# A hybrid encoder layer on eight cores: one explicit order for the mixing stage, transposes moved to DMA, conv statistics by mask matmuls

## The chip, the cores and the metric

The kernel runs on the 8 cores of one Trainium2 chip, each core with one sequence of the batch; the cores exchange nothing. The metric is the device time of the slowest core in microseconds (us). The engines of a core are named as in the profile: PE (TensorE, matmuls), PEld (its weight loads), DVE (VectorE), ACT (ScalarE), POOL (GpSimd) and SP (SyncE, which here only issues DMAs). "SPq" is SP's instruction queue, "POOLq" that of POOL.

## The reference, cut to what matters

One layer over x of 2048 tokens by 1024 channels (per core), with 256 memory tokens:

```python
proj = x @ w_in        # -> conv GLU input 1024 | q 512 | k 128 | v 128 | memory q 512 | gates 3*1024
u = a * sigmoid(g)                                    # branch A: GLU, 512 channels
u = depthwise_conv(u, width 31) + dw_b
u = silu(layer_norm(u over channels, ln_g, ln_b));  y_conv = u @ w_conv_out
# branch B: 8 heads of 64, 2 kv heads, blocks of 128 queries that see 3 blocks of keys
p = softmax([q k^T / 8 + rel_bias, sink])[..., :-1];  y_attn = (p @ v) @ w_attn_out
# branch C: 4 heads of 128 over the 256 memory tokens
y_mem = softmax(q_mem km^T / sqrt(128)) @ vm @ w_mem_out
merged = sum_b sigmoid(gate_b + b_gate) * y_b
x1  = layer_norm(alpha * x + merged @ w_o, ln1)
out = layer_norm(alpha * x1 + (silu(x1 @ w_gate) * (x1 @ w_up)) @ w_ffn_out, ln2)
```

Matmuls run in bf16 with sums in f32.

## The kernel before, in words

The program is written engine by engine with hand-set semaphores: each engine executes its instructions in the order in which the Python code emits them, and a wait at the head of an engine's queue holds all that stands behind it. Inputs live transposed in SBUF (`xT`: channels on partitions), so a projection is a "group": 8 matmuls of 128x128 by 512 tokens into one PSUM bank (`group8`, L333, through the helper `mm`, L221).

Stages, in order:

- **Start.** Small constants are loaded by SP into one slot `s_small`; POOL loads the GLU weights of channel block 0 (`wglu`, gate and value halves in one DMA) and x of token quarter 0 in two halves. The first matmul is that of the attention bias table (`setup_bias`, L412), which waits for all small constants; the GLU groups of quarters 0 and 1 follow, then q, k and v of quarters 0 and 1.
- **Mixing stage**, tokens in four quarters k = 0..3. Its work comes as lists. *Mains*: projection groups (GLU gate `g_gate` and value `g_a`, q, k, v, memory q) and, for output block dp = 0, `c_main`: gate groups `c_gate` and branch projections `c_out`. *W*: windowed attention, per block n three score steps `w_S` (two 64-row matmuls, exp on ACT, bias product on DVE), a value step `w_V` per kv head (12 matmuls of 65 columns, then normalisation on DVE into `otm`), and `w_T` (L618): four PE transposes and a DVE copy into `qT`. *M*: memory attention, units of 512 tokens and one head: `m_S`, `m_V`, and `m_T` (L692): four PE transposes and a copy into `qmT`. *CV*: the conv chain of each quarter: four `conv_c` (L483, 32 matmuls of 32 columns each), `stats` (L503: sums over channels by matmuls with a matrix of ones, which also spreads them over all partitions), mean, variance, `sqrt` on ACT (a table of its own), four `recip` on DVE, `z0` and `fin` (normalise, tanh, product) into `U0`.
- `weave` (L804) and `merge_lists` (L793) mix these lists by weights: a side step is emitted when its share of the sides' weight is reached by the mains' share.
- **Conv inputs.** A conv unit i = 4k + c reads four shifted images of `U0`, made by 16 small DMAs that SP issues (`uq_issue`, L461). There are three buffers: the loads of unit i + 3 are emitted in `conv_c` of unit i and wait for it; they also wait for the GLU output of the next quarter.
- **Gates and outputs** for dp = 1, 2, 3 (`c_main` over four quarters each), nothing else beside them. POOL adds the branches and issues the weight loads; `cache_w1` lets POOL write a bf16 copy of the first FFN weight to HBM, in five large DMAs.
- **Output projection and first LayerNorm** (D): per block of 128 tokens `d_mm` (16 matmuls), `d_H` (residual, DVE, frees the two PSUM banks), `d_S` (sum of squares, ACT), `d_tiny` (DVE), `d_sqrt` (ACT), `d_recip` (DVE), `d_C` (two DVE passes, then a bf16 copy on ACT), `d_Tpe` (L1003: eight PE transposes) and `d_Tev` (L1014: ACT copy into `x1T`). The loop at L1087 interleaves the last of them with the first FFN steps.
- **FFN** (E): `e_step` runs two hidden blocks (32 matmuls; silu on ACT, product on DVE); after 11 steps the second matmul of that quarter follows, which waits for the product of the last block (`e_state["a"]`), then the second LayerNorm and the store.

PSUM has eight banks: during the mixing stage two pairs and four single ones, later a ring of eight.

Of the kernel before, what the change touches and what calls it, by code (L numbers as in the profile page):

```python
# [11 lines left out]
D = 1024  # L12
# [66 lines left out]
class Slot:  # L79
# [11 lines left out]
def _build(plan):  # L91
# [80 lines left out]
    dnt = nc.alloc_sbuf_tensor("dnt", [128, 2, 8], F32)  # L172

# [67 lines left out]
    otm = [V(171.75 + 0.5 * i, [128, 4, 64]) for i in range(4)]  # L241
# [4 lines left out]
    meanb = V(191.75, [128, 512], F32)  # L246
    rstdb = V(193.75, [128, 512], F32)
# [9 lines left out]
    s_small = new_slot("small")  # L257
# [21 lines left out]
    load_glu(0)  # L279
    load_xt(0)  # L280
    load_glu(1)
# [9 lines left out]
    t_eps = pool.run(lambda: nc.gpsimd.memset(eps_t[:, 1:2], 4.0 * LN_EPS))  # L291
    t_onesb = pool.run(lambda: nc.gpsimd.memset(ones_bf[:], 1.0))
# [183 lines left out]
    cst = {"cv": [[], [], [], []], "h": [[], [], [], []], "q": [[], [], [], []], "mean": [], "rstd": []}  # L476
    t_sT = {}

    def conv_steps(k):
# [23 lines left out]
        def stats():  # L503
            b, dd = banks.alloc(2)
            for c in range(4):
                t_a = mm(ps[:, b, :], ones_bf[:], cvh[c], c == 0, c == 3, [S["h", c], t_onesb, dd if c == 0 else None],
                         inc=(c == 3))
            for c in range(4):
                t_b = mm(ps[:, b + 1, :], ones_bf[:], sqb[c], c == 0, c == 3, [S["sq", c]], inc=(c == 3))
            cst["h"] = [[t_a]] * 4  # L510
            cst["q"] = [[t_b]] * 4
            S["mean"] = dve.run(lambda: nc.vector.tensor_scalar(
                out=meanb, in0=ps[:, b, :], scalar1=1.0 / 512, scalar2=None, op0=ALU.mult), [t_a, cst["mean"]])
            t_m2 = dve.run(lambda: nc.vector.tensor_tensor(out=rstdb, in0=meanb, in1=meanb, op=ALU.mult),
                           [S["mean"], cst["rstd"]])
            S["var"] = dve.run(lambda: nc.vector.scalar_tensor_tensor(
                out=rstdb, in0=ps[:, b + 1, :], scalar=1.0 / 512, in1=rstdb, op0=ALU.mult, op1=ALU.subtract), [t_b, t_m2])
            banks.release(b, S["var"], 2)

        def sqrt():  # L520
            S["sd"] = act.run(lambda: nc.scalar.activation(rstdb, rstdb, AF.Sqrt, bias=eps_t[:, 0:1]), [S["var"], t_eps])

        def recip(i):
            S["rs"] = dve.run(lambda: nc.vector.reciprocal(rstdb[:, 128 * i:128 * i + 128], rstdb[:, 128 * i:128 * i + 128]),  # L524
                              [S["sd"]])

        def z0(i):
            S["z0", i] = dve.run(lambda: nc.vector.tensor_tensor(out=cvs[i], in0=cvs[i], in1=meanb, op=ALU.subtract),
                                 [S["mean"], S["h", i]])

        def fin(c):
            t_z1 = dve.run(lambda: nc.vector.tensor_tensor(out=cvs[c], in0=cvs[c], in1=rstdb, op=ALU.mult),  # L532
                           [S["rs"], S["z0", c]])
            cst["rstd"] = [t_z1]
            t_z2 = dve.run(lambda: nc.vector.tensor_scalar(  # L535
                out=cvs[c], in0=cvs[c], scalar1=cvec[:, 4 + c:5 + c], scalar2=cvec[:, 8 + c:9 + c],
                op0=ALU.mult, op1=ALU.add), [t_z1, t_cvec])

            def fin_th():
# [3 lines left out]
                t_th = act.run(lambda: nc.scalar.activation(th2[r], cvs[c], AF.Tanh), [t_z2, th_free[r]])  # L543

                def fin_s():
                    t_sT[k, c] = dve.run(lambda: nc.vector.scalar_tensor_tensor(  # L546
                        out=U0[:, c, 512 * k:512 * k + 512], in0=th2[r], scalar=1.0, in1=cvs[c],
                        op0=ALU.add, op1=ALU.mult), [t_z2, t_th])
# [6 lines left out]
        for c in range(4):  # L555
            steps.append((1.7, lambda c=c: conv_c(c)))
        steps.append((0.1, lambda: None))
# [623 lines left out]
```

How the kernel before makes its waits and increments, by code:

```python
    def wait(self, deps):  # L45
        for tok in _flat(deps):
            if tok[0] == "E":
                _, src, v = tok
                k = id(src)
                if self.seen.get(k, 0) >= v:
                    continue
                self.seen[k] = v
                src.needed.add(v)
                if self.plan is not None:
                    self.eng.wait_ge(src.sem, src.vmap[v])
            else:
                sem, val = tok
                k = id(sem)
                if self.seen.get(k, 0) >= val:
                    continue
                self.eng.wait_ge(sem, val)
                self.seen[k] = val
# [1 line left out]
    def run(self, fn, deps=(), inc=True):  # L64
        self.wait(deps)
        ins = fn()
        if inc:
            self.v += 1
            if self.plan is None or self.v in self.plan[self.name]:
                ins.then_inc(self.sem, 1)
                self.real += 1
                self.vmap[self.v] = self.real
            return ("E", self, self.v)
        return None
# [61 lines left out]
    def dma(e, out, in_, slot, deps=()):  # L136
        e.wait(deps)
        e.eng.dma_start(out=out, in_=in_).then_inc(slot.sem, 16)
        slot.count += 16
        return slot.tok()
```

The softmax here doesn't subtract the row's maximum and nothing guards it: scores larger than these inputs give would overflow.

## Time and profile before

| | us |
|---|---|
| three timed runs, median | 1102.94 (1100.15, 1102.94, 1121.49) |
| the profiled execution, device time | 1101.29 |
| its span on the slowest core, first to last instruction | 1099.7 |
| the eight cores' spans | 1092.8 to 1099.7 |

The profile is of one execution on its slowest core. "Busy" counts time in which an engine executes; issuing a DMA, waiting and branching are not counted. "PEclk" is the granted share of TensorE's full clock. Some 1.6 us of the device time lie outside the span. Stretches of time are counted from the first instruction.

### The profile page before, as it was taken

What the parts mean: (1) busy time and instruction counts of PE and PEld (TensorE: products, weight loads), DVE (VectorE), ACT (ScalarE), POOL (GpSimd) and SP (SyncE); (2) the same over time, 40 slices, a digit from 0 to 9 for tenths busy, and PEclk for the clock granted to TensorE, in tenths of its full rate; (3) what the DMA queues carried; (4) which work ended last, traced back from release to release, by engine and by line L of the source; (5) the groups of instructions that cost most, each with busy time, mean ns of one, the idle gap of its engine ahead of it and who ended that gap; (6) DMA issues with size and microseconds to landing.
All of it is one profiled execution on the core that took longest, in us unless ns stands there. A gap on an engine that the chain in (4) does not pass through costs nothing.

```text
span 1099.7 us, 15676 instructions; the slowest of 8 cores (1092.8 to 1099.7 us)
## 1 busy us (share of the span) xinstructions
PE 1008.7 (92%) x5662; PEld 466.1 (42%) x5662; DVE 434.6 (40%) x789; ACT 359.4 (33%) x518; POOL 124.9 (11%) x156
## 2 busy tenths in 40 slices
PE   3999978546979999999999999999999999999996
PEld 1445434222435444444444444444444444444442
DVE  1325575417587222222235855143213322342224
ACT  1135544415645222222223798122111211121111
POOL 2100000000111433433330010000000000000000
PEclk9999989868989999999999999999999999999998
DMA  9990102550012895973049198405440444134401
GB/s 140 191 187 12 53 22 61 111 119 24 13 32 56 132 171 90 139 120 77 1 86 291 35 206 206 154 39 155 154 152 39 134 153 154 39 117 153 134 19 58
DMA packets 39467, 116.22 MB, mean 106 GB/s; under 512 B 7584, under 2 KB 15912, under 8 KB 38144
## 3 DMA queue, kind: packets, MB, share of 16 engines
q0 software_dynamic: 11136, 49.55, 25.8%
q1 hardware_dynamic: 28256, 65.67, 19.3%
q8 instruction: 47, 0.77, 0.3%
q14 instruction: 28, 0.23, 0.1%
HBM read 138.32 MB, written 19.93 MB: 144 GB/s over the span
## 4 chain that ended last, share of the span: by engine, by line
PE 83%; SPq 5%; DVE 5%; DMA 3%; ACT 3%; issue 2%; DVEq 0%; POOL 0%; ACTq 0%; POOLq 0%
PE ps L221 81%; SPq L138 5%; DMA arena<-arena 1%; DMA esink<-sinkp 1%; DVE arena L977 1%; ACT arena L935 1%; DVE arena L524 1%; DVE arena L532 1%; ACT arena L664 0%; ACT arena L1016 0%; PE ps L625 0%; PE ps L1008 0%; DVE arena L535 0%; DVE arena L956 0%; DVE arena L546 0%
## 5 line engine op out<-in xcount | busy, mean ns | idle before, releaser
L221 PE MATMUL ps<-arena 128*128 128x512 bf16 (+5 forms) x5372 | 989.3, 365 | 41.8 <-DMA arena<-arena 22.4
L221 PEld LDWEIGHTS ps<-arena 128*128 128x128 bf16 (+2 forms) x5372 | 447.6, 99 | 566.3 <-issue 94.6
L1046 DVE TENSOR_TENSOR arena<-ps,arena 128x512 bf16<-128x512 f32 x88 | 60.6, 691 | 201.0 <-PE ps L221 180.3
L768 DVE SCALAR_TENSOR_TENSOR arena<-arena,ps 128x512 f32<-128x512 f32 x96 | 65.9, 686 | 148.7 <-PE ps L221 148.7
L747 ACT ACTIVATE arena<-ps,bgate_sb 128x512 f32<-128x512 f32 x96 | 66.1, 688 | 168.8 <-PE ps L221 168.8
L1044 ACT ACTIVATE arena<-ps 128x512 f32<-128x512 f32 x88 | 51.4, 597 | 180.8 <-PE ps L221 180.7
L935 ACT ACTIVATE arena<-arena 128x1024 bf16<-128x1024 f32 (+1 forms) x32 | 33.9, 1058 | 140.4 <-DVE arena L1067 133.1
L775 POOL TENSOR_TENSOR arena<-arena 128x512 f32<-128x512 f32 x32 | 40.4, 1263 | 199.3 <-DVE arena L768 189.8
L138 POOL DMA_DIRECT2D out<-arena x16 | 8.5, 532 | 411.9 <-DVE arena L958 411.9
L587 ACT ACTIVATE arena<-ps 128x1024 bf16<-128x1024 f32 x46 | 46.8, 1023 | 8.3 <-PE ps L221 8.3
L780 POOL TENSOR_TENSOR arena<-arena 128x512 bf16<-128x512 f32 x32 | 40.8, 1274 | 61.2 <-DVE arena L768 56.6
L1067 DVE SCALAR_TENSOR_TENSOR arena<-arena,ps 128x1024 f32<-128x1024 f32 x16 | 19.5, 1221 | 67.2 <-PE ps L221 67.2
L958 DVE SCALAR_TENSOR_TENSOR arena<-arena,mvt 128x1024 f32<-128x1024 f32 x32 | 41.1, 1285 | 3.6
L956 DVE SCALAR_TENSOR_TENSOR arena<-arena,mvt 128x1024 f32<-128x1024 f32 x32 | 41.0, 1281 | 2.1 <-DVE mvt L952 0.4
L590 DVE TENSOR_TENSOR arena<-arena 128x1024 bf16<-128x1024 bf16 x46 | 35.0, 760 | 14.8 <-ACT arena L587 14.8
L330 ACT CAST arena<-ps 128x512 bf16<-128x512 f32 (+1 forms) x29 | 16.5, 571 | 36.1 <-PE ps L221 36.1
L500 DVE CAST arena<-arena 128x512 bf16<-128x512 f32 x16 | 6.8, 426 | 53.9 <-ACT arena L493 53.9
L977 DVE SCALAR_TENSOR_TENSOR arena<-arena,ps 128x1024 f32<-128x1024 f32 x16 | 19.4, 1212 | 18.3 <-PE ps L221 18.3
L493 ACT ACTIVATE arena<-ps,cvec_sb 128x512 f32<-128x512 f32 x16 | 11.0, 688 | 47.4 <-PE ps L221 47.3
L138 POOL DMA_DIRECT2D arena<-w_g x12 | 6.5, 554 | 154.6 <-PE ps L221 154.6
L948 ACT ACT_TABLE_LOAD x12 | 15.4, 1283 | 23.8 <-DVE mvt L943 23.6
L138 POOL DMA_DIRECT2D arena<-w_f x22 | 11.7, 548 | 100.9 <-PE ps L1008 100.3
(83 smaller groups left out, 369.0 us busy)
## 6 DMA issues: line engine op xcount, KB each, us to landing
arena<-w_bf_cache SPq DMA_DIRECT2D x88, 512.0 KB, 4.0
arena<-arena SPq DMA_DIRECT2D x256, 33.8 KB, 1.9
arena<-x SPq DMA_DIRECT2D x16, 512.0 KB, 21.3
out<-arena POOLq DMA_DIRECT2D x16, 512.0 KB, 2.9
w_bf_cache<-w_f POOLq DMA_DIRECT2D x3, 2560.0 KB, 47.1
arena<-w_g POOLq DMA_DIRECT2D x12, 512.0 KB, 10.2
arena<-w_f POOLq DMA_DIRECT2D x22, 256.0 KB, 8.8
arena<-xt POOLq DMA_DIRECT2D x8, 512.0 KB, 31.0
```

Source lines behind the costliest of these rows:

```text
L138: e.eng.dma_start(out=out, in_=in_).then_inc(slot.sem, 16)
L221: return pe.run(lambda: nc.tensor.matmul(out, lhsT, rhs, start=start, stop=stop), deps, inc)
L587: t_p = act.run(lambda: nc.scalar.activation(flat, bank2(b), AF.Exp, scale=0.125), [tk, PTw_free[rp], btab["t"]])
L747: t = act.run(lambda: nc.scalar.activation(gb[r], ps[:, bk, :], AF.Tanh, bias=bgate[:, b * 8 + dc:b * 8 + dc + 1], scale=0.5), [tk, gb_fre ...
L768: t_y = dve.run(lambda: nc.vector.scalar_tensor_tensor(out=gb[r], in0=gb[r], scalar=1.0, in1=ps[:, bk, :], op0=ALU.add, op1=ALU.mult), [tk ...
L775: c_state["s"] = pool.run(lambda: nc.gpsimd.tensor_tensor(out=gb[r0], in0=gb[r0], in1=gb[r], op=ALU.add), [c_state["y", 0], t_y])
L780: t_mg[dp, tt, dci] = pool.run(lambda: nc.gpsimd.tensor_tensor(out=merged[dp][:, dci, tt * 512:(tt + 1) * 512], in0=gb[r0], in1=gb[r], op= ...
L935: return act.run(lambda: nc.scalar.activation(junk, buf, AF.Square, accum_out=st[:, 1:2]), deps)
L956: te = dve.run(lambda: nc.vector.scalar_tensor_tensor(out=buf, in0=buf, scalar=mv[:, 0:1], in1=tabs[:, 0, :], op0=ALU.subtract, op1=ALU.mu ...
L958: return dve.run(lambda: nc.vector.scalar_tensor_tensor(out=dst, in0=buf, scalar=mv[:, 2:3], in1=tabs[:, 1, :], op0=ALU.mult, op1=ALU.add) ...
L1044: t_s = act.run(lambda: nc.scalar.activation(sgf[sr], ps[:, bG, :], AF.Silu), [tG, sg_free[sr]])
L1046: t_a = dve.run(lambda: nc.vector.tensor_tensor(out=actT[:, j, :], in0=ps[:, bU, :], in1=sgf[sr], op=ALU.mult), [tU, t_s, e_state["dep"]])
```

## The change

It replaces the weaving by a string that gives the order of every step of the mixing stage, one letter each: `a` mains, `w` windowed attention, `m` memory attention, `c` conv chain, `g`, `o`, `k`, `b` weight loads. The list of mains itself is changed too: GLU of quarters 2 and 3 comes before memory q of these quarters, and all four `c_main(0, tt)` are in it. Transposes of both attentions' outputs and of x1 are DMAs, issued by SP (attention) and ACT (x1). The conv LayerNorm forms its statistics with tokens on partitions, inverts them with arithmetic on DVE, transposes six short rows by PE and spreads them by matmuls with a 0/1 mask. The first loads are reordered, the bias table comes after the first GLU pair, D runs all sixteen `d_mm` first, and the second FFN matmul waits block by block. Weights of lists are now unused.

```diff
+ORDER = (
+    "wwawawawkwaawwawawawaawawawwmaaacmwacmcmawkmcwawamcwwamcwawawamcwcwackwcawaccamaakmacaaccmawacaw"
+    "wawccwwcagcagwwagmagwgkcwgagowwwcagcomagmccmaagwagccwmaaacgwcmcokamccwamccaawmamkamcaaccwcwacwaw"
+    "aawacccaamcwccawawcammccwmawmaawcawaawccamcaamaaccaaawamacwaawcmwambaaaaaaaaaaaaa"
+)
...
-    load_glu(0)
+    load_glu(0, 1)
     load_xt(0)
+    load_glu(0, 0)
     load_glu(1)
...
         def stats():
-            b, dd = banks.alloc(2)
-            for c in range(4):
-                t_a = mm(ps[:, b, :], ones_bf[:], cvh[c], c == 0, c == 3, ...)
-            for c in range(4):
-                t_b = mm(ps[:, b + 1, :], ones_bf[:], sqb[c], c == 0, c == 3, ...)
+            b, dd = banks.alloc(1)
+            for blk in range(4):
+                for c in range(4):
+                    t_a = mm(ps[:, b, blk:blk + 1], cvh[c][:, blk * 128:(blk + 1) * 128], ones_bf[:, 0:1], ...)
+            for blk in range(4):
+                for c in range(4):
+                    t_b = mm(ps[:, b, 4 + blk:5 + blk], sqb[c][:, blk * 128:(blk + 1) * 128], ones_bf[:, 0:1], ...)
...
+        def split():
+            S["rs"] = rsqrt(cst_s[:, 1, 0:4], cst_s[:, 0, 4:8], cst_s[:, 2, 0:4], S["v"])
...
+        def tr():
+            for blk in range(4):
+                t_t = pe.run(lambda: nc.tensor.transpose(psb[0:6, b, blk * 128:(blk + 1) * 128], sp3[:, blk, :], ident_bf[:]), ...)
+            S["row"] = dve.run(lambda: nc.vector.tensor_copy(row6[:], psb[0:6, b, 0:512]), [t_t, cst["row"]])
+        def bcast():
+            for i in range(2):
+                t_m = mm(ps[:, b + i, :], msk[:, i, :], row6[:], True, True, [S["row"], dd, t_msk], inc=(i == 1))
+            S["bc"] = act.run(lambda: nc.scalar.copy(mrb.rearrange("p s t -> p (s t)"), bank2(b)), ...)
...
+    def w_V(n):
...
+        t_o = dve.run(lambda: nc.vector.tensor_tensor(out=otm[n % 2], in0=num, in1=rd_b, op=ALU.mult), [t_rc, otm_free[n % 2]])
+        later(1, lambda: w_T(n, t_o))
+    def w_T(n, t_o):
+        t_oT[n] = dma_t(sp, qT[:, :, n * 128:(n + 1) * 128], otm[r].rearrange("p a b c -> p (a b c)"), wt_slot[r], [t_o])
+        otm_free[r] = [t_oT[n]]
...
+    def m_T(u, t_o):
+        t_omT[u] = dma_t(sp, qmT[:, h, tt * 512:(tt + 1) * 512].rearrange(...), omtm[r].rearrange(...), mt_slot[r], [t_o])
+        om_free[r] = [t_omT[u]]
...
+    mains = (qm_list(0) + qm_list(1) + mkv + q_list(2) + kv_list(2) + g_list(2) + g_list(3) + q_list(3) + kv_list(3) +
+             qm_list(2) + qm_list(3) + c_main(0, 0) + c_main(0, 1) + c_main(0, 2) + c_main(0, 3))
+    in_order(ORDER, a=mains, w=cat(W), m=cat(M), c=cat(CV), g=[wg_drip(b, i) ...], o=[wos_drip(b) ...],
+             b=[(1.0, load_b)], k=[(1.0, lambda: cache_w1(1))] * 8)
...
+    def d_T(tb):
+        t_x1T[tb] = dma_t(act, x1T[:, :, tb * 128:(tb + 1) * 128], x1b[r], xt_slot[r], [d_state.pop(("cb", tb))])
+        x1b_free[r] = [t_x1T[tb]]
...
-                                [dO, e_state["w2"], e_state["a"]] if (half == 0 and j == 0) else (),
+                                [dO if j == 0 else None, e_state["w2"], a_tok[j]] if half == 0 else (),
...
+    def d_chain():
+        k = chain["k"]
+        chain["k"] += 1
+        if k + 2 < 16:
+            d_S(k + 2)
+        if k >= 0:
+            d_C(k)
+        if k + 2 < 16:
+            d_tiny(k + 2)
+        if 0 <= k + 1 < 16:
+            d_sqrt(k + 1)
+            d_recip(k + 1)
+        if k >= 0:
+            d_T(k)
+    for tb in range(16):
         d_mm(tb)
+        d_H(tb)
+        if tb >= 2 and tb % 3:
+            d_chain()
+    e_start()
+    si = 0
+    while chain["k"] < 16:
+        d_chain()
+        if chain["k"] > 5:
+            e_step(si)
+            load_w2(9 + 2 * si, min(22, 11 + 2 * si), pe.tok())
+            si += 1
```

`chain["k"]` starts at -2. A function given to `later(1, ...)` is emitted directly after the step that registers it. `dma_t` waits for its operands on the issuing engine and issues one transposing DMA. `fin` keeps one DVE product and moves scale and shift to ACT; there is no `sqrt` and no `recip` of 512 columns in the conv chain any more.

## Rows read from the trace of the kernel before

**Rows 1.** The page's head, and the longest piece of the chain.

```profile
span 1099.7 us, 15676 instructions; the slowest of 8 cores (1092.8 to 1099.7 us)
PE 1008.7 (92%) x5662; PEld 466.1 (42%) x5662; DVE 434.6 (40%) x789; ACT 359.4 (33%) x518; POOL 124.9 (11%) x156
...
360.07 229.66 PE ps L221 x1064
```

**Rows 2.** Stretches: length, busy time of each engine, PEclk, DMA share, GB/s.

```profile
120.00:217.00 97.00, 78.04 (x668) 36.70 (x665) 57.17 (x109) 46.06 (x64) 2.66 (x5) 0.93 0.27 60
217.00:234.00 17.00, 0.60 (x8) 0.34 (x12) 0.00 (x0) 0.00 (x0) 0.00 (x0) 0.55 0.96 170
234.00:302.00 68.00, 56.12 (x482) 26.71 (x472) 40.93 (x80) 35.38 (x46) 5.39 (x4) 0.89 0.09 26
302.00:360.00 58.00, 48.65 (x399) 24.78 (x398) 47.09 (x99) 29.30 (x38) 10.97 (x11) 0.94 0.22 42
...
567.00:625.00 58.00, 54.81 (x292) 25.53 (x290) 38.43 (x78) 26.13 (x42) 2.71 (x6) 1.00 0.69 185
```

**Rows 3.** Timeline at the start; POOL's loads of x, quarter 0.

```profile
16.78 1.86 PE L221 MATMUL ps<-arena,rb 32*8 32x512 f32 x2 [16.78 <-DMA esink<-sinkp]
18.57 41.80 PE L221 MATMUL ps<-arena 128*128 128x512 bf16 x204
...
L138 POOL DMA_DIRECT2D arena<-xt x2: 535/540/546, 2.2 to 2.8; - x2
...
DMA to landing us min/median/max: 11.2/12.6/14.1
```

**Rows 4.** SP's conv loads (ns min/median/max, first and last start) and the chain.

```profile
L138 SPq DMA_DIRECT2D arena<-arena x128: 507/575/3114, 162.8 to 252.8; - x128
...
217.09 16.17 DMA arena<-arena
...
564.44 11.96 SPq L138 DMA_DIRECT2D arena<-x  x12
```

**Rows 5.** PE groups by form: count, busy us, mean ns, idle before.

```profile
L221 PE MATMUL ps<-arena 128*32 128x512 bf16 x512 | 35.6, 427 | 22.4 <-DMA arena<-arena 22.4
L221 PE MATMUL ps<-arena 64*128 64x512 bf16 x92 | 18.4, 395 | 10.9 <-ACT arena L664 9.1 <-DVE arena L687 1.8
L221 PE MATMUL ps<-arena 128*128 128x65 bf16 x368 | 17.6, 198 | 0.1
L221 PE MATMUL ps<-arena 128*128 128x129 bf16 x128 | 10.5, 228 | 2.3 <-ACT arena L587 2.3
```

**Rows 6.** Timeline of D and of the first mixed FFN steps.

```profile
602.30 0.61 PE L1008 MATMUL ps<-ident_bf,arena 128*128 128x128 bf16 x8 [0.33 <-DVE mvt L940]
...
602.75 3.62 PE L221 MATMUL ps<-arena 128*128 128x512 bf16 x16
...
607.03 1.28 DVE L956 SCALAR_TENSOR_TENSOR arena<-arena,mvt 128x1024 f32<-128x1024 f32 x1
...
608.42 1.28 DVE L958 SCALAR_TENSOR_TENSOR arena<-arena,mvt 128x1024 f32<-128x1024 f32 x1
...
609.69 1.20 DVE L977 SCALAR_TENSOR_TENSOR arena<-arena,ps 128x1024 f32<-128x1024 f32 x1
609.79 1.05 ACT L1000 CAST arena<-arena 128x1024 bf16<-128x1024 f32 x1 [0.34 <-DVE arena L958]
...
611.60 0.30 ACT L948 ACTIVATE mvt<-mvt,eps_t 128x1 f32<-128x1 f32 x1 [0.76 <-DVE mvt L943]
...
628.45 1.28 ACT L1044 ACT_TABLE_LOAD   x1
...
629.74 1.09 ACT L1044 ACTIVATE arena<-ps 128x512 f32<-128x512 f32 x2
```

**Rows 7.** The end of an FFN quarter's first matmuls, timeline.

```profile
704.95 0.69 DVE L1046 TENSOR_TENSOR arena<-ps,arena 128x512 bf16<-128x512 f32 x1 [2.76 <-PE ps L221]
705.78 6.42 PE L221 MATMUL ps<-arena 128*128 128x512 bf16 x29 [1.01 <-DVE arena L1046]
```

More of the change, by code:

```diff
@@ L240, in _build @@
     PTm = [V(167.75 + 2 * i, [128, 2, 512]) for i in range(2)]
-    otm = [V(171.75 + 0.5 * i, [128, 4, 64]) for i in range(4)]
+    otm = [V(171.75 + i, [128, 2, 4, 64]) for i in range(2)]
     omtm = [V(173.75 + i, [128, 4, 128]) for i in range(2)]
@@ L514, in stats @@
[L514 to L521, printed above, removed]
@@ L539, in fin_th @@
+            cst["bfree"] = [t_z1]
             def fin_th():
@@ L618, in w_T @@
[L618 to L631 removed]
+        b, dd = banks.alloc(2)
@@ new lines, in w_V @@
+        for g in range(2):
+            for h in range(4):
+                for i, (kblk, rp, t_b) in enumerate(res):
+                    tk = mm(ps[:, b + g, h * 128: h * 128 + 65], PTw[rp][:, g, h * 128:(h + 1) * 128],
+                            vaug[:, kblk, g, :], i == 0, i == len(res) - 1,
+                            [t_b, dd, t_v[kblk // 4], t_vones] if g + h == 0 else (),
+                            inc=(g == 1 and h == 3 and i == len(res) - 1))
+        for (kblk, rp, t_b) in res:
+            PTw_free[rp] = [tk]
@@ new lines, in w_V @@
+        t_rc = dve.run(lambda: nc.vector.reciprocal(rdn, dn), [t_dn])
+        rd_b = bass.AP(rdt, rdn[:, 0:1].offset, [[rdt[:].ap[0][0], 128], [4, 2], [1, 4], [0, 64]])
+        t_o = dve.run(lambda: nc.vector.tensor_tensor(out=otm[r], in0=num, in1=rd_b, op=ALU.mult), [t_rc, otm_free[r]])
+        banks.release(b, t_o, 2)
+        later(1, lambda: w_T(n, t_o))
+    wt_slot = [new_slot("wt") for _ in range(2)]
+    def w_T(n, t_o):
+        r = n % 2
+        t_oT[n] = dma_t(sp, qT[:, :, n * 128:(n + 1) * 128], otm[r].rearrange("p a b c -> p (a b c)"), wt_slot[r], [t_o])
+        otm_free[r] = [t_oT[n]]
@@ L899, in _build @@
     t_wo = load(w_o_sb, w_o_d, [a_done])
-    cache_w1(5)
-    weave(cat([c_main(2, tt) for tt in range(4)]), [])
+    cache_w1(3)
+    straight(cat([c_main(2, tt) for tt in range(4)]))
     dp2_done = pe.tok()
-    cache_w1(4)
     w1_tok = {}
@@ L920, in load_w1 @@
         w1_tok[i] = dma(sp, w1s[r], w1b_d[seq[i][1]], w1_slot[r], [w1_free[r], w1c["t"]])
-    weave(cat([c_main(3, tt) for tt in range(4)]), [])
+    straight(cat([c_main(3, tt) for tt in range(4)]))
     c_done = pe.tok()
@@ L927, in _build @@
         load_x(tb, [c_done, t_mg[3, 3, 1]])
-    for i in range(3):
-        load_w1(i)
+        if 6 <= tb < 9:
+            load_w1(tb - 6)
     load_w2(0, 9, [c_done, t_mg[3, 3, 1]])
```

377 lines of the change are left out of this document (169 added, 208 removed).

## The prediction

> **What bounds the kernel now.** I read the page's head first: PE is busy 1008.7 of 1099.7 us, so what is to be won is PE's idle time of 91 us and any matmul that goes. The stretches tell where the idle time lies [rows 2]. From 120 to 360 us, in the mixing stage, PE lacks 19.0, 16.4, 11.9 and 9.4 us, 56.7 in all, and its granted clock falls to a mean of 0.55 in the worst of these stretches. Around D it lacks 3.2. The chain then holds one piece of 1064 matmuls in 229.66 us [rows 1], 0.216 us each, with no wait: 72 of c_main(0, 3), 864 of the other three output blocks, 128 of D. That stretch can't gain, and it dates the stages: c_main(0, *) ends at 360.07 + 72 x 0.216 = 375.6.
>
> What ends the waits of the mixing stage is SP. It issues the conv loads without a pause from 162.8 to 252.8 us, 128 of them, eight units of 16 [rows 4]: 0.575 us is the median of one issue, and start to start it is 90.0 / 127 = 0.709. A conv unit thus costs SP between 16 x 0.575 = 9.2 and 16 x 0.709 = 11.3 us; I take 10.2, the middle, since large weight loads beside them (the landing that the chain shows took 16.17 us) are now cut small. The reader should see that POOL, ACT and DVE have room on average in these rows and SP, which they don't list, has none.
>
> **The change, part by part.** The sum is made against the profiled execution's 1101.3 us, 1.6 below the median of the runs.
>
> *PE work.* 256 transposes of 128 columns go. Eight start 0.45 us before the next matmul [rows 6], so x1's 128 are worth 7.2 us and the attentions' 128 as much. The conv statistics swap 32 matmuls of 512 (6.9) for 128 of one column, 16 small transposes and eight of 512. The nearest row to one column is that of 65, 17.6 / 368 = 0.048 us [rows 5]: 6.1 + 0.9 + 1.7 = 8.7. I take no gain or loss there; at the spacing of 512 columns it would be +23, with nothing for the narrow ones -4.3.
>
> *Start.* Before, the bias matmul waits to 16.78 and the first group starts at 18.57 [rows 3]. Now the groups come first. The second half of x landed at 2.8 + 14.1 = 16.9; with half a weight block less ahead of it the value group can start then, with the gate group done, and the bias matmul's 1.9 us follow. I take 2.5 us; ends 0 and 5. By the groups that follow, the part that the string orders starts near 67.
>
> *Mixing stage: a ledger of PE against SP.* PE prices [rows 1, 5]: projection group 1.73, conv unit 35.6 / 16 = 2.2, score step 18.4 / 46 = 0.40, value step 17.6 / 16 = 1.1, memory score 0.43, memory value 10.5 / 16 = 0.66, branch projection 0.86. Summed over the string these give 243 us, so with no wait at all the stage would end at 310. SP prices: 10.2 a unit, 2 us to landing as a guess; for a transposing DMA the trace has no row. Its ends are the shortest and longest conv issue, 0.5 and 3.1 us [rows 4]; x's loads of 128 partitions took 11.96 / 12 = 1.0. I take 0.8 for attention's (between 0.575 and 1.0) and 1.0 for x1's, twice as large.
>
> Up to conv unit 0 the string holds 29.3 us of PE: 96.3. Unit 3's loads follow it and land at 110.7, when PE is just there. 18.7 us later, at 129.4, the GLU value of quarter 2 exists, and with DVE's part SP can begin unit 4 at 130. From here SP is the clock:
> - Units 4 to 7 and two transposes: 130 + 40.8 + 1.6 = 172.4, landed 174.4. PE is at unit 7 36.6 us after 129.4, at 166: it waits 8.
> - Two transposes and units 8 to 10: to 204.6. Only then comes the transpose of block 7, emitted right after unit 7 but behind these loads; it lands at 207.4. Block 9 uses the same `otm` buffer. Its product waits for this landing on DVE, and behind it all of DVE: bias products, evacuations, normalisations. PE passes block 9 at 193, can go on for 4 us (four steps whose banks ACT frees or that are still free) and stops: 10 us. This is a new wait.
> - Then 13 us of PE to unit 8 (221), unit 11 is loaded 223.4 to 233.6 and lands at 235.6; PE needs it at 230.6: 5 us.
> - One transpose, units 12 to 14, five transposes, unit 15: 234.4 + 30.6 + 4.0 + 10.2 = 279.2, landed 281.2, needed at 277.1: 4 us.
> - 57.4 us of PE remain: 338.6, against 375.6. This part gives -37.0, start and 128 transposes included.
>
> On that path lie 12 units and 11 transposes of SP. With 9.2 and 0.5 the stage would end at 323, with 11.3 and 3.1 at 377. POOL's loads in pieces I cost at nothing, as they lie beside PE work; at the end of the stage the last memory transpose shares the DMA engines with the next weights, and if it lands as late as 16 us [rows 4] the branch projection that reads it, some 9 us later, waits 7.
>
> *D and the first FFN steps.* Before, each step of the loop was transposes, d_mm and 0.34 idle; D's 16 d_mm, its transposes, 3.2 idle and 21 FFN units of 16 matmuls come to 55.3 + 7.2 + 3.2 + 72.5 = 138.2. After: d_C is two DVE passes, 607.03 to 609.69, ACT's copy 1.05, square root 0.30, d_recip [rows 6]: 4.4 us from one d_recip to the next, in which DVE can't pass. From block 5 to 15 DVE has 11 d_H of 1.3 and seven such chains: 20.8 + 14.4 + 30.8 = 66.0, PE is done at 55.3. PE does not stop yet, as a d_mm needs the banks of four blocks before. Then each FFN step is ringed by: product 0.75, d_C 2.7, copy 1.05 and 0.17 of waits, a table load for the root 1.28, root 0.30, the DMA issue on ACT, a table load back 1.28, two silu 1.1 [rows 6]: 8.6 us and the issue, where PE needs 6.9. Before, the root stood ahead of the copy's wait, so this ring was shorter. First silus at 73.9, seven full rings, one without root (5.75), nine issues: 140.1 + 9 x 1.0 = 149.1, and PE, four units ahead at most, is then at unit 21. +10.9; with 0.5 a piece +6.4, with 3.1 +29.8.
>
> *Ends of FFN quarters.* PE waited 704.95 to 705.78 for the last product [rows 7]; four times 0.83 go as the last block is now read last: -3.3. The per-block waits fall on products that are long done; without that cover a wait would cost its queue step, which no row prices; between 0 and the whole 3.3.
>
> Sum: 1101.3 - 37.0 + 10.9 - 3.3 = 1071.9, 1072.
>
> The trace shows that an issue grows with the transfer (0.575 against 1.0) [rows 4]. The Trainium skill, page "DMA: Bandwidth & Descriptors", section "Why a DMA increments its semaphore by 16 and not by 1", says for chips before its newest that a transpose within SBUF was pushed tile by tile, with 262,144 sequencer cycles for 8,192 tiles; by that rule the issue goes with size, and x1's costs twice an attention's. No row here shows a transpose.
>
> **The rivals.**
> 1. *Transposes are dear to issue.* Place: SP between conv units, and ACT inside the ring of the FFN steps. The stages change by -37.0 + 11 (t - 0.8) + 1.9 + 9t - 3.3 = -47.2 + 20t: slower from t = 2.36. At 3.1, 1101.3 + 14.8 = 1116. For it: ACT and SP are already the clocks of these stretches. Against: a plain issue of that size takes 1.0. 0.12.
> 2. *SP does not hold PE.* The string's gaps between conv units suffice, the stage ends at 310: 1101.3 - 65.6 + 10.9 - 3.3 = 1043; without the ring in D too, 1022. Against it: 9.2 us a unit at the least, and the first burst of four units spans 36 us. 0.20.
> 3. *Issue goes with size*, 0.8 and 1.6: +16.3 in D, 1077. 0.10.
> 4. *The order moves waits without removing them.* Units cost 11.3 as before: the stage ends 13 later, 1085. For: the same bytes travel beside them. 0.20.
>
> **How the numbers follow.** The forecast has 0.38, its own range 1058 to 1086. Range: rivals 1 and 2 reach 1116 and 1022; with a tenth left out at either side 1038 to 1108. About 2% (1081 and 1123) is what a measurement of this kernel tells from no change. Faster: 0.28 of the forecast, all of rival 2, 0.05 of 3, 0.04 of 4: 0.57. Slower by over 2%: 0.05, out of rival 1. The same: 0.38.
>
> **What would show it.** Right: SP's conv loads without a pause from about 130 on; a DVE wait of over 10 us for an attention transpose near 200; waits of PE for conv loads of 4 to 8 us at units 7, 11 and 15; the conv chain's DVE work smaller with no square root table; FFN steps of 9 to 10 us while x1 is still normalised; no wait at the ends of FFN quarters. Wrong: idle PE under 15 us before the output blocks (rival 2), issues of over 2 us on ACT or SP (rival 1), or FFN steps of 6.9 from the first on.

## The result, and the profile after

The changed kernel is slower: 1164.51 us median, against 1112.22 for the kernel before in the same comparison; the ratio is 1.055 (95% interval 1.047 to 1.062; it is formed from undisturbed runs alone, hence not that of the two medians). The forecast was 1072, its range 1038 to 1108.

The profiled execution took 1163.6 us, 62.3 more than that of before. Three boundaries, dated by VectorE's products, tell where they lie. All figures are those of the profiled, slowest core; behind them stands the median of the eight cores, since the cores differ.

| | before | forecast (before, with its terms) | after |
|---|---|---|---|
| end of c_main(0, *) | 376.5 (372.0) | 339.5 | 410.5 (406.7) |
| the three other output blocks | 186.5 | 186.5 | 186.5 |
| D and the first FFN quarter's products | 142.6 (142.7) | 153.5 | 175.3 (155.0) |
| all that follows, to the end of the span | 394.1 | 390.8 | 389.4 |

So +34.0 in place of -37.0, then +32.7 in place of +10.9, and -4.7 in place of -3.3; their sum, 62.0, is the difference of the spans. The page's head, and the packets of the queues of SP (q1) and ACT (q10):

```profile
span 1161.7 us, 15497 instructions; the slowest of 8 cores (1131.6 to 1161.7 us)
...
PE 1001.5 (86%) x5526; PEld 456.1 (39%) x5526; DVE 403.0 (35%) x756; ACT 344.2 (30%) x499; POOL 138.0 (12%) x181
...
q1 hardware_dynamic: 45664, 69.87, 21.2%
q10 hardware_dynamic: 16896, 4.20, 5.6%
```

Each of PE, DVE and ACT has less to do than in [rows 1], and the kernel is slower: the answer lies in waits. The stretches that hold them (columns as in [rows 2]):

```profile
60.00:120.00 60.00, 41.36 (x305) 19.89 (x304) 14.70 (x28) 21.48 (x29) 0.00 (x0) 0.83 0.83 136
170.00:220.00 50.00, 35.20 (x370) 16.33 (x358) 18.93 (x53) 20.44 (x27) 5.80 (x11) 0.90 0.38 75
220.00:280.00 60.00, 32.57 (x305) 17.05 (x306) 17.40 (x33) 19.99 (x28) 3.84 (x7) 0.77 0.57 93
340.00:420.00 80.00, 54.10 (x291) 24.63 (x290) 28.19 (x47) 24.02 (x32) 22.36 (x24) 0.83 0.50 88
```

PE lacks 18.6 us in the first of them and 25.9 in the last. The line that issues the transposing DMAs (issue in ns min/median/max, first and last start; then who waited for their landing), and the three pieces of the chain of waits that are such a DMA:

```profile
L279 SPq DMA_TRANSPOSE arena<-arena x32: 1174/1184/25658, 77.0 to 370.5; - x32
L279 ACTq DMA_TRANSPOSE arena<-arena x16: 1232/1360/9324, 622.0 to 761.2; - x16
...
  DVE arena L675: 34.7, 2
  PE ps L229: 25.3, 1
```

```profile
77.00 32.06 DMA arena<-arena
...
230.40 2.44 DMA arena<-arena
...
367.74 28.10 DMA arena<-arena
```

The medians are ordinary, 1.18 and 1.36 us; the maxima are not. The first transpose holds SP for 25.66 us and lands 32.06 us after its start; the one of block 15, the last but one, lands after 28.10. L675 is the normalisation in the window attention's value step, which writes `otm`: it waits twice: block 2 waits 18.4 us up to 109 until block 0's transpose has landed, and block 9 waits 16.3 up to 232.9 for that of block 7. The L229 wait of 25.3 us is the branch projection at 396. In the normalisation loop, two consecutive FFN steps on ACT:

```profile
686.20 1.04 ACT L1049 CAST arena<-arena 128x1024 bf16<-128x1024 f32 x1 [2.59 <-DVE mvt L988]
...
687.26 1.28 ACT L996 ACT_TABLE_LOAD   x1
687.32 2.07 ACTq L279 DMA_TRANSPOSE arena<-arena  x1
688.56 0.29 ACT L996 ACTIVATE mvt<-mvt,eps_t 128x1 f32<-128x1 f32 x1
...
689.47 1.28 ACT L1083 ACT_TABLE_LOAD   x1 [0.62 <-PE ps L229]
...
690.77 1.08 ACT L1083 ACTIVATE arena<-ps 128x512 f32<-128x512 f32 x2
...
695.48 1.04 ACT L1049 CAST arena<-arena 128x1024 bf16<-128x1024 f32 x1 [2.59 <-DVE mvt L988]
...
696.60 9.32 ACTq L279 DMA_TRANSPOSE arena<-arena  x1
...
706.30 1.28 ACT L1083 ACT_TABLE_LOAD   x1 [8.16 <-issue]
707.59 1.09 ACT L1083 ACTIVATE arena<-ps 128x512 f32<-128x512 f32 x2
...
708.44 8.41 PE L229 MATMUL ps<-arena 128*128 128x512 bf16 x32 [9.47 <-ACT arena L1083]
```

From cast to cast (686.20 to 695.48) it is 9.28 us. The forecast had a ring of 8.6 and the issue on top; but the issue runs beside the table load and the root, and only what is left of its 2.07 us holds ScalarE. From the silu at 690.77 to that at 707.59 it is 16.8: the issue took 9.32, the table load and silu stand behind it, and PE waits 9.47. Four of sixteen issues were held so here (8.95, 9.32, 8.91, 6.86). They are not the same on all cores. Core 0 of the same execution, and the start of one of its steps and of the next:

```profile
L279 ACTq DMA_TRANSPOSE arena<-arena x16: 1247/1249/7796, 615.4 to 732.0; - x16
...
696.96 1.28 ACT L996 ACT_TABLE_LOAD   x1
697.02 1.25 ACTq L279 DMA_TRANSPOSE arena<-arena  x1
...
705.64 1.28 ACT L996 ACT_TABLE_LOAD   x1
```

There a step takes 8.68 us with the issue in it. One issue was held, and D with the first quarter took 151.9. The held one is that of D's second block; it is held on all eight cores, for 7.8 to 10.4 us. Five cores lie between 151.9 and 155.6, three at 167.2, 172.8 and 175.3; the time is that of the slowest.

### The profile page after: what moved, and what is told of

It reads as the page before. It is cut to its first block, busy times and chain, and to the rows that moved or that the text cites. A ratio compares the mean times of both kernels' runs of the same rounds, so it can differ in the third digit from the quotient of the medians.

```text
span 1161.7 us, 15497 instructions; the slowest of 8 cores (1131.6 to 1161.7 us)
## 1 busy us (share of the span) xinstructions
PE 1001.5 (86%) x5526; PEld 456.1 (39%) x5526; DVE 403.0 (35%) x756; ACT 344.2 (30%) x499; POOL 138.0 (12%) x181
## 3 DMA queue, kind: packets, MB, share of 16 engines
q1 hardware_dynamic: 45664, 69.87, 21.2%
## 4 chain that ended last, share of the span: by engine, by line
PE 71%; DMA 9%; SPq 8%; issue 4%; DVE 3%; ACT 2%; ACTq 1%; POOL 0%; DVEq 0%; POOLq 0%
PE ps L229 71%; SPq L144 7%; DMA arena<-arena 7%; DMA arena<-w_bf_cache 2%; DMA arena<-xt 1%; ACTq L279 1%; DVE arena L1004 1%; DVE arena L1006 1%; ACT arena L1049 1%; SPq L279 1%; DVE arena L589 0%; ACT arena L596 0%; ACT arena L1083 0%; DVE arena L647 0%; DVE arena L675 0%
## 5 line engine op out<-in xcount | busy, mean ns | idle before, releaser
L229 PE MATMUL ps<-arena 128*128 128x512 bf16 (+5 forms) x5372 | 994.7, 368 | 149.5 <-DMA arena<-arena 62.3
L229 PEld LDWEIGHTS ps<-arena 128*128 128x128 bf16 (+2 forms) x5372 | 451.4, 100 | 691.3 <-issue 218.1
L1106 DVE SCALAR_TENSOR_TENSOR arena<-arena,ps 128x1024 f32<-128x1024 f32 x16 | 19.5, 1221 | 62.4 <-PE ps L229 62.4
L647 DVE TENSOR_TENSOR arena<-arena 128x1024 bf16<-128x1024 bf16 x46 | 31.9, 701 | 23.4 <-ACT arena L644 23.3
L144 POOL DMA_DIRECT2D arena<-w_g x21 | 11.3, 542 | 205.0 <-PE ps L229 203.0
L1049 ACT CAST arena<-arena 128x1024 bf16<-128x1024 f32 x16 | 16.7, 1044 | 47.8 <-DVE mvt L988 40.3
L675 DVE TENSOR_TENSOR arena<-ps,rdt 128x512 bf16<-128x512 f32 x16 | 11.1, 691 | 37.0 <-DMA arena<-arena 34.7
## 6 DMA issues: line engine op xcount, KB each, us to landing
arena<-x SPq DMA_DIRECT2D x16, 512.0 KB, 25.7
arena<-w_f POOLq DMA_DIRECT2D x22, 256.0 KB, 16.3
```

Of the source, the lines that this page charges most:

```text
L144: e.eng.dma_start(out=out, in_=in_).then_inc(slot.sem, 16)
L229: return pe.run(lambda: nc.tensor.matmul(out, lhsT, rhs, start=start, stop=stop), deps, inc)
```

## The experiments

The theory after these rows: a DMA that carries an intermediate result is held up, in its issue and its landing, while bulk loads are in flight, and the engine that issues it and those that wait for it stand. The first rival: SP's load and ScalarE's ring are the loss by themselves. What the runs gave (total: median of all runs; boundaries: profiled core, median of eight cores in brackets; ratios to before with intervals):

| run | total | ratio | end of c_main(0) | 3 blocks (median) | D, first quarter |
|---|---|---|---|---|---|
| e1 | 1103.59 | 0.996 (0.993 to 0.999) | 353.1 (350.0) | 186.5 | 172.9 (153.4) |
| e4 | 1139.67 | 1.033 (1.030 to 1.036) | 405.4 (399.7) | 186.5 | 150.6 (147.3) |
| e2 | 1147.05 | 1.040 (1.038 to 1.043) | 412.6 (408.3) | 186.5 | 159.0 (158.2) |
| e7 | 1074.23 | 0.974 (0.972 to 0.976) | 354.2 (349.9) | 186.6 | 142.7 (142.7) |
| f1 | 1138.49 | 1.032 (1.030 to 1.035) | 382.6 (381.2) | 186.5 | 178.7 (159.6) |
| e5 | 1150.47 | 1.042 (1.034 to 1.049) | 384.9 (381.4) | 197.4 | 182.8 (154.4) |
| f3 | 1088.77 | 0.989 (0.987 to 0.990) | 356.7 (352.5) | 196.1 | 142.7 (142.7) |
| s8 | 1088.40 | 0.988 (0.986 to 0.989) | 368.4 (364.0) | 186.5 | 143.0 (143.0) |
| g1 | 1146.21 | 1.038 (1.029 to 1.047) | 391.0 (388.0) | 186.5 | 169.9 (155.3) |
| g2 | 1077.52 | 0.978 (0.975 to 0.980) | 349.8 (346.9) | 188.2 | 142.7 (142.7) |
| f4 | 1079.44 | 0.980 (0.978 to 0.982) | 348.4 (348.4) | 192.6 | 143.0 (143.0) |
| g3 | 1068.84 | 0.972 (0.970 to 0.973) | 355.2 (345.4) | 186.5 | 142.7 (142.7) |
| h1 | 1095.98 | 0.996 (0.995 to 0.997) | 354.2 (350.5) | 186.5 | 164.3 (162.9) |

**e1, attention back on TensorE.**

```diff
-        t_oT[n] = dma_t(sp, qT[...], otm[r]..., wt_slot[r], [t_o])
+        for c4 in range(4):
+            t_tr = pe.run(lambda: nc.tensor.transpose(psb[:, b, ...], of[:, ...], ident_bf[:]), ...)
+        t_oT[n] = dve.run(lambda: nc.vector.tensor_copy(qT[...], src), [t_tr])
...
-        later(1, lambda: w_T(n, t_o))
+        later(4, lambda: w_T(n, t_o))
```

The same for the memory units.

> Attention's 32 transposes go back to TensorE (four steps after the product they read), x1's 16 stay DMAs; order, narrow statistics and everything else as after. Theory 1 (transposing DMAs are held up while bulk transfers are in flight, and block SP's queue): the 33 us hole at 73 to 109 us, the 18 us waits near 215 to 233 and the 25 us wait at 396 go; c_main(0) ends near 345 to 355 instead of 410.5; total 1098 to 1112. Theory 2 (the order's own demand on SP is what PE waits for, the transposes are incidental): SP saves 32 x 1.2 us at most, c_main(0) ends no earlier than 390, total 1143 to 1155.

The stage ends 57 us earlier on both measures: theory 1's numbers. The 32 DMAs are the whole loss of the mixing stage. In the rest, D and the first quarter, nothing changed on the median core (153.4 after 155.0). The totals of e1's ten runs lie between 1090.9 and 1116.1, so its ratio of 0.996 does not tell it from before.

**e4, plain DMAs in their place.** The edit replaces `dma_start_transpose` by `dma_start` with the same bytes; the kernel leaves out the transposing.

> All 48 transposing DMAs replaced by plain DMAs of the same bytes, from the same engine at the same place with the same waits; what is left out of the computation is the transposing of the attention outputs and of x1. Theory 1a (it is the transposing that is held up): issues of 0.6 to 1.0 us everywhere, the first one too, c_main(0) ends near 345 to 355, FFN steps 8.7 us without the 16 us ones, total 1080 to 1100. Theory 1b (any small DMA behind the bulk loads is held up so): issues and landings of 25 to 30 us remain, total 1155 to 1170. Theory 2: 1145 to 1160.

Neither 1a nor 1b holds throughout, and the total lies in none of the three ranges. The line of all DMAs that SP and ACT issued between SBUF places, two pieces of the chain, and ACT's queue:

```profile
L144 SPq DMA_DIRECT2D arena<-arena x288: 464/575/18539, 31.2 to 363.2; - x144
...
L144 ACTq DMA_DIRECT2D arena<-arena x16: 601/602/4341, 617.0 to 730.8; - x16
```

```profile
76.96 31.72 DMA arena<-arena
...
362.25 28.91 DMA arena<-arena
```

```profile
q10 hardware_dynamic: 16640, 4.20, 1.7%
```

In the mixing stage the plain DMA suffers as the transposing one did: 31.72 us to landing at the same place, 28.91 at the end, and the stage ends only 7 us earlier on the median core. What costs there is that a DMA carries the tile at all, not that it transposes; the plain one too carries it in small pieces, (39008 - 28256) / 32 = 336 packets a tile (SP's queue in e4 and in e1), and a DMA with few large packets was not tried. On ACT it is the other way: the issue is 0.60 in place of 1.23, one is held on this core, for 4.3 us, and D with the first quarter takes 150.6, 24.7 less than after. There the transposing matters, on the median core by 7.7 us (147.3 after 155.0). Where issues were held its packets also occupied the DMA engines longer: 5.6% of 1161.7 us, 65 us of all sixteen engines, against 1.7% of 1131.9, 19 us, for the same 4.20 MB; on core 0 of after, with one held issue, it was 2.4% of 1131.6, 27 us. Undisturbed, the two hardly differ in landing: 3.1 us after the start of the issue and 2.9.

**e2, x1 back on TensorE in the new loop; e7, all transposes on TensorE and the old loop of D.** e2 adds the eight transposes and ScalarE's copy two chains later; e7 takes e1 and the loop of before.

> x1's 16 transposes go back to TensorE with ScalarE evacuations, in the new order of the normalisation chain (each two chains after its copy); attention still by DMA. Theory 1: the four 7 to 9 us issues on ScalarE and what they delay go, the ring of 8.6 us stays: steps of 8.5 to 9.5 us, D and first FFN quarter 175 to 152 us, total 1138 to 1146. Rival (the ring through copy, root and table loads alone is the loss): steps keep lengths up to 16 us, total 1158 to 1168. Third possibility, no ring: steps of 6.9, total near 1131.

> All transposes back on TensorE and the loop of D and the first FFN steps as in before; kept of the change: the order string, the narrow statistics, the start, the loads in pieces, the late wait of the last FFN product. Theory 1: c_main(0) ends at 345 to 355, D and first FFN quarter 142 us as before, quarters 1 us shorter: total 1062 to 1080. Theory 2: 1105 to 1120.

e2 shows the ring without held issues: steps of 9.5 us, 157.5 to 159.0 in all on the eight cores, against 142.7 with the old loop in e7. The new loop costs 16.3 by itself where a copy of 0.99 us stands in its ring, 7 more than theory 1 allowed; the total lies 1 us above its range. e7 is 2.6% faster than before. From its page, and PE's waits for DMAs within SBUF up to the stage's end, in after and in e7 (us in total, times, longest):

```profile
PE 1006.3 (94%) x5782; PEld 467.2 (44%) x5782; DVE 411.3 (38%) x777; ACT 364.5 (34%) x526; POOL 137.8 (13%) x181
...
PE ps L229 <- DMA arena<-arena: 62.3, 6, 25.3
...
PE ps L229 <- DMA arena<-arena: 21.9, 3, 8.3
```

**f1, four buffers of the window output in place of two.**

```diff
+    otm += [nc.alloc_sbuf_tensor(f"otm{i}", [128, 2, 4, 64], BF16)[:] for i in (2, 3)]
...
-        t_o = dve.run(... out=otm[r] ..., [t_rc, otm_free[r]])
+        t_o = dve.run(... out=otm[n % 4] ..., [t_rc, otm_free[n % 4]])
```

> As after, but four buffers in place of two for the window attention's output ahead of its transposing DMA. Theory (the product of block n+2 waits on VectorE for the landing of block n's transfer, which SP can't deliver: at 73 to 110 us behind bulk loads, near 200 behind the conv loads of units 8 to 10): the first hole shrinks from 18.6 us to the 2 to 9 us that the run with TensorE transposes shows, the wait near 215 to 233 goes, the 25 us wait at the stage's end stays; c_main(0) ends at 370 to 382, total 1122 to 1138. Rival (the blocked queue only moves the wait to later blocks or to the conv loads behind the transposes): c_main(0) ends after 395, total over 1147.

The stage ends 25.5 us earlier on the median core, and no value step waits for a window buffer any more (one of the memory units' waits 8.0). The end stays as it was:

```profile
337.43 30.01 DMA arena<-otm
```

The two places where DVE stood were thus a matter of two buffers. The total, and c_main(0) on the profiled core, lie half a us above their ranges; held issues made D 178.7 on that core.

**e5, the weight loads at the stage's end wait for the last transposes; f3, this with four buffers and the old loop of D.**

```diff
-        load_wg(1, [[t_sT[3, c] for c in range(4)]])
+        load_wg(1, [[t_sT[3, c] for c in range(4)], t_oT[15], t_omT[15]])
```

> As after, but the weight loads that POOL starts at the end of the mixing stage wait until the last two attention transposes have landed. Theory (these transposes land 28 us after their issue only because those loads are in flight): they land 2.4 us after their issue, the 25 us wait of the branch projection goes, c_main(0) ends at 384 to 390, total 1135 to 1143. Rival (the weights are then late in their place, or the transposes are slow by themselves): less than 10 us gained, total over 1152.

> Four buffers, the late weight loads, and x1 on TensorE with the loop of D as before; attention's 32 transposes stay DMAs. If the three places (two buffers, the bulk loads at the end, ScalarE's ring with its held issues) are all that the DMA transposes cost, c_main(0) ends at 342 to 358 and the total is 1062 to 1080, no worse than with all transposes on TensorE (1074). If the DMA transposes cost SP's queue something else, the total stays over 1090.

The chain of e5, and PE's wait after that:

```profile
370.81 2.44 DMA arena<-arena
...
375.40 20.22 DMA arena<-w_out
...
PE ps L229 <- DMA arena<-w_out: 10.0, 1, 10.0
```

Half right. Without the loads beside it the last transpose lands in 2.44 us, and c_main(0) ends where expected. But the weights are then late: the three output blocks take 11 us more. The rival had named that, the theory's total had not counted it; the total lies between the two ranges. f3 shows the same: its stage ends at 356.7, its blocks take 9.6 more, and the total missed its 1080.

**s8, the wide statistics again, on top of e7.** `stats`, `sqrt` and `recip` of before in the same steps of the order.

> All transposes on TensorE as in the run e7, and the conv chain's statistics as before (32 matmuls of 512 columns with ones, square root on ScalarE, reciprocal of 512 columns on VectorE) in the same places of the order. The prediction costed the narrow statistics at nothing: total 1068 to 1080 by that. If the shorter VectorE work or the missing table loads are worth something here, 1080 to 1095; if the longer chain of small steps cost more than it saved, under 1068.

The narrow statistics are worth 14.2 us, not nothing; the stage's end moves by as much (368.4 and 354.2). The stage in e7 and in s8 (columns as in [rows 2]), and the wide matmuls of s8:

```profile
0.00:354.20 354.20, 301.16 (x2427) 144.99 (x2428) 164.64 (x361) 158.27 (x215) 49.42 (x82) 0.96 0.52 88
...
0.00:368.40 368.40, 307.98 (x2307) 145.37 (x2308) 172.77 (x309) 166.96 (x223) 49.43 (x82) 0.94 0.48 85
...
L229 PE MATMUL ps<-arena,ones_bf 128*128 128x512 bf16 x32 | 7.6, 378 | 2.3 <-DVE arena L645 1.5 <-ACT arena L692 0.8
```

The narrow ones, in the profile of after:

```profile
L229 PE MATMUL ps<-ones_bf,arena 128*128 128x1 bf16 x128 | 3.8, 163 | 0.3 <-DVE dnt L670 0.3
L229 PE MATMUL ps<-row,msk 6*128 6x512 bf16 x8 | 2.4, 378 | 0.0
L570 PE MATMUL ps<-ident_bf,sp 128*6 128x128 bf16 x16 | 1.5, 219 | 0.0
```

At one column they take 0.030 us each, not the 0.048 of [rows 5]. But the three groups make 7.7 us, and the wide ones 7.6: on PE the statistics themselves gain nothing. Of the 14.2, 7.4 are PE's waits: from 20 us to the stage's end those for DVE and ACT rise from 16.9 in e7 to 29.5, those for DMAs fall from 21.9 to 16.8. The other 6.8 are a longer busy time of PE on the rest of its work, with a mean granted clock of 0.94 of full speed in the stage where e7 has 0.96.

**g1, the early weight copies moved.** The string issues five copies of FFN weights with no wait of their own, so POOL reaches them at 38 us, right behind the bulk loads.

```diff
-    "wwawawawkwaawwawawawaawawawwmaacmwacmcmawkmcwawamcwwamcwawawamcwackcwkcawaccamaakmacaaccmawacaw"
+    "wwawawawwaawwawawawaawawawwmaacmwacmcmawmcwawamcwwamcwawawamcwaccwcawaccamaamacaaccmawacaw"
...
-    cache_w1(4)
+    cache_w1(6)
```

> As after, but the first five copies of FFN weights into the cache, which the order string issues at 38 us behind the bulk loads, move into the copies beside the three output blocks (6, 6, 4 there in place of 4, 4, 3). Theory (a DMA from SP lands only when the bulk ahead of it has drained): the first transpose lands 10 to 25 us earlier than 109, the hole of 18.6 us at 91 shrinks to 0 to 8, c_main(0) ends 8 to 18 us earlier (392 to 402), total 1146 to 1157. Rival (the copies are not what holds the queue, or a transposing DMA needs 25 us at its first use): first landing within 3 us of 109, c_main(0) at 408 to 413, total 1160 to 1166.

The DMA engines and the software queue between 60 and 105 us: before, after, and g1 (busy tenths of 40 slices; packets, MB, share).

```profile
DMA  9989999999999999982000000000000000000011
...
q0 software_dynamic: 705, 2.99, 36.7%
```

```profile
DMA  9999999998999999999999205980596009915905
...
q0 software_dynamic: 978, 6.46, 93.7%
```

```profile
DMA  9998999998999999999999980500000041000021
...
q0 software_dynamic: 844, 4.01, 48.3%
```

Before, the engines were full to 80 us and then idle. After, they are full to 85 and then work in bursts to the end: the copies. The software queue's packets take 93.7% of the stretch. In g1 it is quiet from 87 on; the first transpose is issued at 80.4 and held for 2.23 us, and PE is busy 57.3 of the 60 us to 120, not 41.4. The stage ends 19 us earlier, 1 us below what was expected. The first transpose is not slow for being the first: the rival falls.

The Trainium skill, page "DMA: Bandwidth & Descriptors", section "Queues, rings and completion order", says that each DMA engine goes round its queues one packet at a time. The trace of after shows the turns: while the first transpose was in flight the two queues moved packets one for one as long as there was bulk (84 to 102 us), and the rest of SP's, conv loads and transposes together, followed as it ended (102 to 108):

```profile
q0 software_dynamic: 138, 2.21, 95.1%
q1 hardware_dynamic: 139, 0.10, 2.1%
...
q1 hardware_dynamic: 1788, 0.76, 58.9%
q0 software_dynamic: 28, 0.20, 16.2%
```

By this section of the Trainium skill, as an estimate, a small transfer pays a bulk packet for each of its own: the 32 transposes brought 45664 - 28256 = 17408 packets (SP's queue in after and in e1), 34 on each engine for one, and a turn of the software queue took 45 x 0.937 / (978 / 16) = 0.69 us, so one transpose needs some 23 us beside bulk. The 32.06 measured, with conv loads ahead of it, is more, and e4's plain DMAs, 336 / 16 = 21 packets on each engine, landed as late. The count of packets thus does not price the landing here; it follows the end of the bulk.

**g2, the copies moved so on top of e7; f4, four buffers, the copies moved, the last three transposes on TensorE; g3, the copies at the last conv unit.**

> All transposes on TensorE, loop of D as before, and the five copies moved as in the run before this one. Theory: the third conv unit's loads, which landed near 109 us behind the bulk, come earlier, and up to 9 us of TensorE's waits at 91 to 120 go; c_main(0) at 345 to 353, total 1063 to 1071. Rival: the conv units behind it set the time, the copies are worth nothing: 1072 to 1077.

> Attention's DMA transposes kept where they can hide: four window buffers, copies moved, the last window block and the last two memory units on TensorE, weight loads as in after, x1 on TensorE in the loop of before. If the DMA transposes' cost was collisions and buffers, c_main(0) ends at 338 to 350 and the total is 1056 to 1070, at or below the run with all transposes on TensorE. If SP as the clock of the conv loads pays for each of the 29 DMAs, c_main(0) ends at 355 to 365, total 1075 to 1085.

> All transposes on TensorE and the loop of D as before, with the five early weight copies moved to the last conv unit (TensorE there near 288 us), where the DMA engines are idle until the loads at 334. Theory: the gain of the run g2 in the mixing stage without what it lost beside the output blocks: c_main(0) ends at 347 to 352, the three other output blocks take 186.5 us as in after, total 1066 to 1072. Rival (the copies then delay the weight loads of 334): the end of c_main(0) or of the next block is 5 or more us later, total 1074 to 1082.

In g2 and f4 the stage ends as expected, and both totals miss: beside the output blocks the moved copies made other loads late, 5.3 us of waits in g2 and 8.4 in f4 on the profiled cores. g3 puts them, with a wait on PE's count, where nothing else moves:

```diff
-    "aawacccaamcwccawawcammccwmaw..."
+    "aawacccaamcwccawawckkkkkammccwmaw..."
...
-             ... k=[(1.0, lambda: cache_w1(1))] * 8)
+             ... k=[(1.0, lambda: cache_w1(1, [pe.tok()]))] * 8)
```

It is the fastest of all, 2.8% under before, though its interval still touches that of e7. The profiled core missed the boundary expected (355.2; the seven others lie between 342.1 and 346.5). f4 keeps 29 DMA transposes, most of them hidden; its stage ends no earlier than that of g2 without one (348.4 and 346.9).

**h1, thirteen loads at once.** The second FFN weight's loads, two a step in e1, come all at the first step.

```diff
-            load_w2(9 + 2 * si, min(22, 11 + 2 * si), pe.tok())
+            if si == 0:
+                load_w2(9, 22, pe.tok())
```

> Attention on TensorE and x1 by transposing DMAs, as in the run e1 (D and first FFN quarter 172.9 us there), but the 13 loads of the second FFN weight that came two a step all come at the first step. Theory (transposing DMAs on ScalarE's queue are held while bulk loads share the DMA engines): issues of over 4 us only in the some 20 us after the first step, at most one; those at the fourth to ninth step back at 1.2 to 2 us; D and first quarter 160 to 167 us, total 1090 to 1098. Rival (a transposing DMA is held by those before it on its own queue, or by the first weight's loads from SP): as many long issues as in e1, total 1100 to 1106.

```profile
606.88 6.87 POOL L144 DMA_DIRECT2D arena<-w_f  x13 [59.44 <-PE ps L229]
```

```profile
614.58 11.54 ACTq L279 DMA_TRANSPOSE arena<-arena  x1
```

The hold follows the loads. On the profiled core it begins 7.7 us after the first of them, and the eight issues behind it take 1.25 to 1.44. Each of the eight cores has one such issue of 10.1 to 12.0 us, and D with the first quarter takes 159.9 to 165.3 on all of them; the median, 162.9, is 9.5 above that of e1. In e1 the profiled core was held at four of these steps, up to 12.0, two others for up to 5.3, and five at none (2.2 at most). The first weight's loads and the queue's own earlier transfers were the same in both runs; so the rival falls.

## Why the prediction was wrong, step by step

- **PE bounds, SP ends its waits in the mixing stage.** Right. In after PE waited for conv loads at the units named, 7, 11 and 15, for 10.0, 13.7 and 9.9 us (forecast 8, 5 and 4). The ledger's form held once the new DMAs were gone: e7 ends the stage at 354.2, 14.7 over the forecast, with 7 us of transposes in it that the forecast had not, and 21.9 of waits for conv loads, at units 2, 7 and 11.
- **The step that failed: "2 us to landing as a guess", with 0.8 an issue, for attention's transposes.** The usual values were near (2.4 and 1.18). But I used them for every transpose, where a row of mine showed a conv load landing in 16.17 us beside weights [rows 4]. Beside bulk loads a landing took 28 to 32 us and an issue up to 25.66. By e1 the 32 DMAs cost 57 us. Undone singly on the median core, their places give: two buffers 25.5 (f1), loads beside the last ones 25.3 (e5), copies beside the first 18.7 (g1), of which f1 and g1 share the hole of 18.6 us that begins at 91.
- **"POOL's loads in pieces I cost at nothing."** Wrong, 18.7 us in the mixing stage (g1), though nearly all of it through the transposes that landed late: without DMA transposes the same move is worth 3.0 (g2 after e7, median core). I read the order string as if a letter's place were its time. A step on an engine that has nothing to wait for runs at once, and five `k` ran at 38 us.
- **"If it lands as late as 16 us ... waits 7", costed at nothing.** The mechanism was right, at the place named, for the last window transpose as for the last memory one (landed after 28.10 and 25.7); PE waited 25.3.
- **The wait of block 9 on `otm`.** Right: forecast near 200, landing at 207, 10 us; measured until 232.9, 16 us of PE. f1 removes it. The same dependence at block 2, with bulk in place of conv loads ahead of it, I did not look for.
- **The start, 2.5 us.** Nearly nothing came: the projections ahead of the string end at 68.4 us, before at 68.8 (median of eight cores).
- **Conv statistics "no gain or loss".** Right for their matmuls, 7.7 us after 7.6, though in part by luck: the narrow ones took 0.030 us each, not 0.048, the transposes and the mask matmuls more than forecast. Wrong for the whole by 14.2 us to the good (s8), half waits and half PE's busy time at another clock, for which the sum had no term.
- **The ring in D: 8.6 us and the issue.** The ring is right, 8.68 measured where nothing is held. The issue on top of it is wrong: it runs beside the root's table load, and e4's steps, with issues of 0.60 in place of 1.25, take 8.68 too. The forecast's +10.9 was thus too much: e4, where little is held, lies at +4.6 on the median core. That the median core of after stands at 155.0, near the forecast's 153.5, is luck: the held issue of the second block, which the forecast had not, fills the gap. The loss above it, 20 us, is issues held later; "1.0 for x1's" is the second term that failed. They fall on some cores, and the slowest sets the time.
- **Ends of quarters, -3.3.** Right: -4.7 for four, 1.2 each in place of 0.83.
- **Rivals.** "Transposes are dear to issue" named both places, but by its formula even the mean issue of 2.1 us on SP and 3.2 on ACT gives about the time of before; what it lacked is the landing. That issue goes with size: 1.18 for 128 KB on SP and 1.23 for 256 KB on ACT undisturbed, so it does not, against the rule that I had cited for it. "SP does not hold PE" fell with e7.

Left open: why a transposing issue is held on ACT where a plain one mostly passes; why three cores of eight are hit; and the shares of the order and of the loads in pieces. s8, which has these, the start and the late FFN wait, lies 13.5 us under before, 4.7 of it the FFN wait.

## What to carry to other kernels

Before a tile on the path goes from an engine to a DMA, look at what else the DMA engines carry at that minute, and price it by the nearest landing beside bulk, not by the quiet one; give it more buffers than landings in flight. In an order written out by hand, a load's place means nothing unless the load waits for something. Read more than one core: a delay that strikes some cores and not others counts in full, as the slowest sets the time. And where a forecast is met, look whether its terms are: two wrong ones can cancel.

## What the runs showed of the hardware

- A DMA of 128 KB within SBUF, in 544 or 336 packets, landed in 2.0 to 2.5 us undisturbed and in 28 to 32 beside bulk loads, transposing (after) or not (e4); the issue held SP for up to 25.66 and 18.54 us.
- SP's queue and the software queue moved 139 and 138 packets in the same 18 us of after, though these make 0.10 MB and 2.21; 1788 of SP's followed in the next 6.
- A transposing DMA of 256 KB, undisturbed, took 1.23 us to issue and landed after 3.1, a plain one 0.60 and 2.9. Beside loads the transposing issue was held for up to 13.1 us (after, all cores), the plain one for up to 4.6 (e4). The Trainium skill, page "Advanced Engine Details and Errata", section "X-Bar Transpose (TRN2)", says that transposing DMAs are as fast as regular ones; by the undisturbed landing these runs nearly agree, by the issue and by the holds they do not.
- An issue of 1.25 us on ACT ran beside a table load of 1.28 and cost its queue nothing: steps with issues of 0.60 were as long, 8.68.
